# First modulation weights loaded ahead, and the start of the first layer put in another order: a fused two-layer hybrid block on one core

## The chip, the cores and the metric

The kernel runs on one core of a Trainium2 chip. Its time is device microseconds from one execution, and lower is better. Three executions of the kernel before gave 1947.54, 1946.19 and 1947.12 us, so the median is 1947.12 us. TensorE (PE in the profile, PEld for its weight loads) does the matmuls, VectorE is DVE, ScalarE is ACT, GpSimd is POOL, and SyncE is SP. SP and ACT issue the DMAs.

## The reference, cut to what matters

The network has two layers over 256 context tokens and 256 latent tokens of width 1024, all in float32. Each layer first makes its normalised input `h` and then feeds four mixers. The change touches only what is computed before the first projection of layer 0, so this is what matters:

```
mod   = silu(c)     @ w_ada[li] + b_ada[li]      # (6*1024): shift1, scale1, gate1, shift2, ...
mod_c = silu(c_ctx) @ w_ada[li] + b_ada[li]
h  = rmsnorm(x,  norm1[li]) * (1 + scale1)  + shift1
hc = rmsnorm(xc, norm1[li]) * (1 + scale1c) + shift1c
p, pc = h @ w_in[li], hc @ w_in[li]              # 1024 x 5648

# filter of the Hyena branch, per layer, orders n = 0, 1: depends on weights alone
hdn  = sin(freq0 * (feats @ w1 + b1));  hdn = sin(freq1 * (hdn @ w2 + b2))
taps = (hdn @ w3).reshape(256, 2, 2, 512) * decay        # both directions
taps = taps / sum(abs(taps), axis=0)
kf   = rfft(taps, n=512)
```

## The kernel before, in words

The activations of both streams lie transposed in SBUF, as `xT`: 8 blocks `k` of 128 channels by 512 tokens (context, then latent). A projection is done in strips: a strip is 512 rows by 256 columns of a weight matrix (512 KB), loaded by SP into one of four slots of `raw`, split by ACT (`split_hi`, L1535) and by DVE or POOL (`split_lo`, L1544) into a high and a low part in one of two slots of `whl`, and multiplied in three products (high by high, low by high, high by low; `mm3`, L660). So `h` too has a high and a low part, `hhl`. All other matmuls (L655) and the transposes through the identity (L760, L766) are plain float32. An order of the work is written out by hand for each engine; engines meet at semaphores, and each runs its own list in order. PSUM has eight banks: four `unit` banks and four `work` banks, which `fill` hands out in turn; `fill` waits until the consumer of the bank four fills before has given it back.

The start of layer 0 is `start_` on PE, ACT and DVE, then `norm(0, 0)`, then `dn(0)`, whose first twelve strips (`feature_strips`, L660) need `h`. In `start_` there are three pieces of work:

- The first eight modulation groups. A group `g` is 256 columns of `w_ada[0]`, all 1024 rows, loaded as two strips through the four slots of `raw`. `mod_group(0, g)` multiplies `csil` (the two conditioning vectors through SiLU) by both strips, in eight matmuls that use 32 columns of the array each. ACT copies the result to `modrow` (`mod_row`), PE transposes it (`mod_turn`, L760), and DVE reduces it into `mod` and adds the bias (`mod_cols`). There is one `modrow`, so the groups follow one another. `amps` makes the scale of the norm from groups 4 to 7.
- The activations: `stage` holds `ctx` and `x`; PE transposes them into eight fills and ACT copies these to `xT`. POOL squares seven of the eight blocks and adds them up (L3397, L3399), ACT squares the last, PE sums over the channels with two products by ones, and ACT makes `rstd`. `norm(0, 0)` then builds `hn` = x * amp * rstd: DVE the even blocks in one operation per stream (L2750), POOL the odd ones in two steps, the scale (L3405) and `rstd` (L3432). ACT adds the shift and rounds to the high part (L1783), DVE makes the low part (L2739). `h_ready` counts the blocks, and PE waits for it block by block in the first two strips.
- The filter of both orders `n` of layer 0: `filter_angles` (two small products, each followed by nine DVE operations and a sine), `filter_taps` (four products of 64 rows by 512 columns, with DVE's `filter_cut` behind), `filter_sums` (sums and differences of the directions, DVE), ACT's absolute values (`filter_taps` on ACT), `filter_scale` (four products by ones, and a reciprocal on DVE), `filter_spectrum` (eight products) and `filter_nyquist` (two). For order 1 the spectrum stands behind the norm and the last two products inside the first strips of `dn(0)`, at chunk 4 of `between`.

Rows of the biases, norms, convolutions and of `c` and `c_ctx` are loaded by SP and transposed together in `columns(li)` (L815, L817). SP loads first these rows, then the constants, then the modulation strips as slots come free, with `ctx` and `x` behind strip 3. ACT's queue loads the small filter operands at the very start and the three large filter tables (`hy_w3`, `decay`, the first part of `hy_table`) after the first `modrow` copy (L1816).

The lines that end the start, as they stand before:

```python
            start_()
            for li in range(DEPTH):
                norm(li, 0)
                if li == 0:
                    filter_spectrum(0, 1)
                dn(li)
```

Of the kernel before, what the change touches and what calls it, by code (L numbers as in the profile page):

```python
# [20 lines left out]
P = 128  # L21
# [99 lines left out]
def build(nc, x, c, ctx, c_ctx, w_ada, b_ada, norm1, norm2, w_in, attn_qk_gain, attn_lambda, attn_subln,  # L121
# [3 lines left out]
    with es:  # L125
# [33 lines left out]

        whl = sbr("whl", [P, RING, 2, KS, STRIP])  # L160
        hhl = sbr("hhl", [P, 2, KD, T])
# [98 lines left out]

        f_w1, f_w2, f_s, f_arg, f_turns, f_feats, f_inv = carve((P,), (P,), (L,), (L,), (L,), (L,), (BR_W,), at=6144)
# [36 lines left out]
        ROWS_DONE = [7 * 16, 5 * 16]  # L298
        HYW = 3 * 16
        HALF = L // 2 + 1  # L300
        FILTER_SMALL, FILTER_LARGE = 11 * 16, 3 * 16
# [73 lines left out]
        def qk_tile(li, which, m_):  # L375
            if which and li:
# [9 lines left out]
        hyf_loaded = sem("hyf_loaded")  # L386
# [5 lines left out]
        vm_loaded = [sem(f"vm_loaded{i}") for i in range(4)]  # L392
        unit_done = sem("unit_done")
# [8 lines left out]
                 "exp_ready a_ready aT_ready turns_ready odd_ready eo_ready anti_ready hyk_ready hyf_clear hyf_arg hyf_sin hyf_cut hyf_sums hyf_taps z_ready zf_ready hy_u fn_u fn_v "  # L402
# [35 lines left out]
        at_unit = at_mark = 0  # L438
# [104 lines left out]
        FIRST_MODS = 2 * D // STRIP  # L543
# [8 lines left out]
        add_mods(0, range(FIRST_MODS))  # L552
# [37 lines left out]
        def turn_bank(li, g):  # L590
            return unit_bank[first_unit[("mod", g), li] % UNITS][:, STRIP:2 * STRIP]
# [17 lines left out]
        def _(pe):  # L609
# [133 lines left out]
            def mod_group(li, g):  # L743

                assert first_strip[("mod", g), li] == n_strip[0]
                bank = fill(("mg", li, g)) if in_work_bank(li, g) else unit()
                for kh in range(2):
# [4 lines left out]
                    m.then_inc(filled if kh and in_work_bank(li, g) else unit_done, 1)  # L752
                if 0 < mod_place(li, g) < FIRST_MODS:
                    mod_turn(li, g - 1)
# [14 lines left out]
            def filter_angles(i):  # L769
                if i == 0:  # L770
                    pe.wait_ge(hyf_loaded, FILTER_SMALL)
                    b = fill(("f1",))
                    mm(b[:, 0:L], f_w1[0:HY_EMB, :], f_feats[0:HY_EMB, :]).then_inc(filled, 1)
                else:
                    pe.wait_ge(S["hyf_sin"], 1)
                    b = fill(("f2",))
# [20 lines left out]
            def filter_spectrum(li, n):  # L797
                z = f_z0[li][n]
                for fc in range(4):
# [12 lines left out]
            def columns(li):  # L812
                pe.wait_ge(rows_loaded[li], ROWS_DONE[li])
                b = fill(("cols", li))
                nc.tensor.transpose(b[:, 0:100], rows_of[li][0:100, 0, :], ident[0:100, 0:100])  # L815
                n = 52 if li == 0 else 36
                nc.tensor.transpose(b[:, 128:128 + n], rows_of[li][0:n, 1, :], ident[0:n, 0:n]).then_inc(filled, 1)  # L817

            def start_():
                pe.wait_ge(consts_loaded, 16)  # L820
                columns(0)
                filter_angles(0)
                pe.wait_ge(S["cT_ready"], 2)
                for g in range(FIRST_MODS):
                    mod_group(0, g)
                    if g == 0:
                        filter_angles(1)
# [9 lines left out]
                    if g == 4:  # L837
                        filter_scale(0, 0)
# [2782 lines left out]
```

## Time and profile before

| | |
|---|---|
| median of three runs | 1947.12 us (1946.19 to 1947.54) |
| span of the profiled execution, first to last instruction | 1946.3 us |
| PE busy over the span | 1873.7 us (96%) |
| DVE, ACT, POOL busy | 1284.9, 788.5, 608.5 us |
| mean granted clock of TensorE over the span | 0.987 |

The profiled execution is known only by its span; what lies around the span in a run is not listed for it. A row of the timeline gives start, duration, engine, line, operation, output<-input, shape and count, and in brackets the idle time before with what ended it. One float32 matmul stands as two records in the rows of L655. A granted clock of 1.00 is 2.4 GHz and 0.50 is 1.2 GHz.

### The profile page before, as it was taken

To read this page: it belongs to the slowest core of one execution; us is meant where nothing else is said; L and a number is where in the kernel's file an instruction comes from. 1 tells how busy PE (TensorE), PEld (TensorE's weight loads), DVE (VectorE), ACT (ScalarE), POOL (GpSimd) and SP (SyncE) were. 2 spreads that over 40 slices of the span, in tenths; PEclk is the share of its full clock that TensorE was granted. 3 is DMA by queue.
4 is the path that set the end of the run, shared out by engine and by line. 5 is a ranking of instruction groups with operands and counts; after the bars stand their busy time and mean duration, and the time that the engine had idled before them with its cause. 6 is when DMAs were issued, how large, how long until landed. Compare 5 with 4: busy or idle time off the path is not lost.

```text
span 1946.3 us, 32006 instructions
## 1 busy us (share of the span) xinstructions
PE 1873.7 (96%) x11146; PEld 1525.9 (78%) x11146; DVE 1284.9 (66%) x2122; ACT 788.5 (41%) x1627; POOL 608.5 (31%) x553
## 2 busy tenths in 40 slices
PE   6999899999999999999999999999998899999999
PEld 2556788767588888877888887787787789999999
DVE  4754867666856755358765776759686655567574
ACT  2325633356243333333222232356535545445453
POOL 3433243722312111163200223444555521143030
PEclk8999899999999999999999999999999999999999
DMA  6433111232234443344555556233214335554554
GB/s 226 139 107 105 38 56 55 87 121 80 84 130 152 130 161 118 95 134 160 185 173 186 174 194 196 87 87 87 77 44 136 104 109 176 177 168 156 180 183 140
DMA packets 210925, 252.98 MB, mean 130 GB/s; under 512 B 11715, under 2 KB 176900, under 8 KB 209796
## 3 DMA queue, kind: packets, MB, share of 16 engines
q1 hardware_dynamic: 207088, 235.01, 38.2%
q10 hardware_dynamic: 3732, 16.60, 2.3%
q8 instruction: 61, 1.00, 0.2%
q14 instruction: 44, 0.36, 0.1%
HBM read 245.29 MB, written 6.29 MB: 129 GB/s over the span
## 4 chain that ended last, share of the span: by engine, by line
PE 73%; issue 10%; DVE 8%; POOL 5%; ACT 4%; DMA 1%; ACTq 1%; DVEq 0%; POOLq 0%
PE psum L660 58%; PE psum L655 13%; POOL whl L1544 2%; DVE big L2570 2%; PE psum L766 1%; POOL big L3537 1%; ACT whl L1535 1%; ACT big L1783 1%; ACT big L1786 1%; PE psum L628 1%; DVE hhl L2739 1%; DVE big L2579 1%; POOL big L1634 1%; DMA big<-in_hy_table_dram 1%; DVE big L2722 1%
## 5 line engine op out<-in xcount | busy, mean ns | idle before, releaser
L660 PE MATMUL psum<-hhl,whl 128*128 128x512 f32 (+1 forms) x4416 | 826.6, 346 | 11.6 <-DVE hhl L2739 4.3
L660 PEld LDWEIGHTS psum<-hhl,whl 128*128 128x128 f32 x4416 | 693.3, 190 | 132.4 <-issue 24.8
L1535 ACT CAST whl<-raw 128x512 fp32r<-128x512 f32 x656 | 374.1, 618 | 811.6 <-PE psum L660 806.6
L1544 DVE TENSOR_TENSOR whl<-raw,whl 128x512 fp32r<-128x512 f32 x480 | 333.6, 736 | 315.3 <-ACT whl L1535 314.4
L660 PE MATMUL psum<-bigr,whl 128*128 128x512 f32 (+1 forms) x2688 | 474.9, 337 | 1.5 <-DVEq L3314 0.7
L660 PEld LDWEIGHTS psum<-bigr,whl 128*128 128x128 f32 x2688 | 412.8, 190 | 57.2 <-issue 2.2
L1544 POOL TENSOR_TENSOR whl<-raw,whl 128x512 fp32r<-128x512 f32 x176 | 233.6, 1349 | 377.5 <-ACT whl L1535 359.0
L655 PE MATMUL psum<-big 128*128 128x128 f32 (+8 forms) x1572 | 245.7, 326 | 17.9 <-DMA big<-in_hy_w_dram 5.4
L655 PEld LDWEIGHTS psum<-big 128*128 128x128 f32 (+4 forms) x1572 | 164.5, 175 | 77.3 <-issue 51.8
L3537 POOL TENSOR_TENSOR big<-big,tmp 128x512 f32<-128x512 f32 (+1 forms) x64 | 64.5, 1021 | 341.3 <-DVE tmp L3311 340.7
L660 PE MATMUL psum<-whl,hhl 128*128 128x512 f32 x672 | 160.1, 396 | 11.0 <-POOL whl L1544 9.1
L660 PEld LDWEIGHTS psum<-whl,hhl 128*128 128x128 f32 x672 | 125.6, 190 | 40.1 <-POOL whl L1544 12.2
L1786 ACT COPY big<-psum 128x512 f32<-128x512 f32 (+3 forms) x182 | 90.3, 497 | 131.3 <-PE psum L655 93.3
L1596 POOL TENSOR_TENSOR tmp<-tmp 128x512 f32<-128x512 f32 (+1 forms) x32 | 31.3, 979 | 320.1 <-ACT tmp L1783 320.1
L2722 DVE SCALAR_TENSOR_TENSOR big<-big,csil 128x512 f32<-128x512 f32 x112 | 87.9, 785 | 5.2
L1783 ACT ACTIVATE big<-psum 128x512 f32<-128x512 f32 (+3 forms) x142 | 65.9, 475 | 26.3 <-PE psum L655 10.8
L3405 POOL TENSOR_SCALAR big<-xT,amp 128x256 f32<-128x256 f32 x48 | 54.3, 1143 | 37.9 <-issue 26.7
L2703 DVE SCALAR_TENSOR_TENSOR big<-big,csil 128x512 f32<-128x512 f32 x84 | 64.4, 819 | 1.8 <-DVE tmp L3311 1.8
L2570 DVE TENSOR_TENSOR big<-psum,big 128x512 f32<-128x512 f32 (+2 forms) x74 | 47.5, 642 | 22.1 <-PE psum L655 19.1
L2574 DVE TENSOR_SCALAR big<-psum,cols 128x512 f32<-128x512 f32 (+1 forms) x48 | 31.8, 662 | 45.1 <-PE psum L660 27.0
L2579 DVE SCALAR_TENSOR_TENSOR big<-psum,cols,big 128x510 f32<-128x510 f32 (+1 forms) x96 | 58.4, 608 | 2.6
L1783 ACT ACTIVATE big<-psum,small 128x512 f32<-128x512 f32 (+2 forms) x72 | 40.8, 594 | 39.8 <-DVE small L2576 21.7
(187 smaller groups left out, 1524.9 us busy)
## 6 DMA issues: line engine op xcount, KB each, us to landing
raw<-in_w_mlp_dram SPq DMA_DIRECT2D x128, 512.0 KB, 3.8
raw<-in_w_in_dram SPq DMA_DIRECT2D x88, 512.0 KB, 3.7
big<-in_w_ada_dram SPq DMA_DIRECT2D x88, 512.0 KB, 5.1
raw<-in_w_gate_dram SPq DMA_DIRECT2D x64, 512.0 KB, 3.5
raw<-in_w_branch_dram SPq DMA_DIRECT2D x32, 512.0 KB, 3.5
raw<-in_w_ada_dram SPq DMA_DIRECT2D x24, 512.0 KB, 5.3
raw<-in_w_o_dram SPq DMA_DIRECT2D x16, 512.0 KB, 3.5
hy_spectra<-big ACTq DMA_DIRECT2D x2, 2560.0 KB, 9.3
```

The source lines that it names most:

```text
L655: return nc.tensor.matmul(o_, a, b, start=start, stop=stop)
L660: m = nc.tensor.matmul(o_, a(p_), b(q_), start=first and i == 0, stop=last and i == 2, skip_group_check=shared)
L1535: nc.scalar.copy(whl[:, r, 0, ks], raw_of(n)[:, ks]).then_inc(S["hi_ready"], 1)
L1544: ins = eng.tensor_tensor(whl[:, r, 1, ks], raw_of(n)[:, ks], whl[:, r, 0, ks].bitcast(F32), ALU.subtract)
L1783: return nc.scalar.activation(o_, i_, fn, **kw)
L1786: return nc.scalar.copy(o_, i_)
L2570: step(V.tensor_tensor(o_, a, b, op), s_)
L2579: step(V.scalar_tensor_tensor(o_, a, sc, b, op0, op1), s_)
L2703: V.scalar_tensor_tensor(um_acc[:, r, :] if k == 7 else um_part[:, r, :], um_raw[k // 2][:, k % 2, :], csil[:, k, r:r + 1], um_part[:, r, ...
L2722: ins = V.scalar_tensor_tensor(vm_acc if k == 7 else vm_part, w, c_, vm_part, MUL, ADD)
L3405: ins = G.tensor_scalar(hn[:, k, sl], xT[:, k, sl], amp[:, li, which, k, s_:s_ + 1], None, ALU.mult)
L3537: G.tensor_tensor(m_acc[:, i, tk], m_acc[:, i, tk], tmp[:, i % 2, tk], ALU.add)\
```

## The change

- The weights of the eight groups are loaded whole and ahead, into places that are unused until then: groups 0 and 1 as one transfer of 2 MB (512 columns, 1024 rows) into a part of the arena (where `hn` comes later), 2 and 3 into the memory of `whl`, 4 and 5 into the first half of `hhl`, 6 and 7 as two transfers of 1 MB into the rest of `hhl`. They no longer pass through `raw`. `mod_group(0, g)` becomes `first_mod(g)`.
- SP's list begins with the constants, `ctx` and `x`; the three filter tables are issued by SP among the modulation weights. The rows of both layers are issued by ACT's queue.
- `c` and `c_ctx` are loaded by ACT's queue into `tmp` and transposed on their own, ahead of all else on PE.
- The squares of all eight blocks are made by ACT into `raw`, and POOL only adds them. PE sums over the channels with one product, in the middle of the groups, and `rstd` is made there. The first two strips of `dn(0)` and groups 6 and 7 are loaded after that sum is done.
- The four absolute blocks of the taps of each order are added by POOL (`filter_added`), so that `filter_scale_added` has one product in place of four.
- A group's transposition (`mod_turn`) stands behind another piece of PE's work, not directly behind the next group.
- Both spectra of layer 0, and both `filter_nyquist`, are now on PE within `start_`; the one inside `dn(0)` goes.
- `first_norm` takes the place of `norm(0, 0)`: POOL multiplies the odd blocks by `rstd` before the last groups are there, and then scales and shifts them in one operation; the rest is as before.
- ACT's store of the first spectra (`keep_spectra(0)`) stands two steps later in `dn(0)`.

```diff
@@ PE @@
+            def first_mod(g):
+                bank = unit()
+                at, c0 = mod_part(g)
+                pe.wait_ge(mod_loaded[min(at, 3)], 16 if at < 3 else 32)
+                for k in range(KD):
+                    m = mm(bank[32 * (k % 4):32 * (k % 4) + 32, 0:STRIP], csil[:, k, :],
+                           mod_raw[at][:, k, c0:c0 + STRIP], k < 4, k >= 4)
+                m.then_inc(unit_done, 1)
+            def filter_scale_added(n):
+                pe.wait_ge(S["hyf_added"], n + 1)
+                mm(fill(("fs", 0, n)), ones, f_z1[0][n][:, 0, :]).then_inc(filled, 1)
             def start_():
                 pe.wait_ge(consts_loaded, 16)
+                pe.wait_ge(crow_loaded, 32)
+                nc.tensor.transpose(fill(("c",))[:, 0:16], crow, ident[0:16, 0:16]).then_inc(filled, 1)
+                filter_angles(0)
+                pe.wait_ge(x_loaded, 32)
+                for k in range(KD):
+                    b = fill(("x", k))
+                    turn(b, [stage[:, m, k * P:(k + 1) * P] for m in range(NT)]).then_inc(filled, 1)
+                filter_angles(1)
                 columns(0)
+                columns(1)
+                filter_taps(0, 0)
                 pe.wait_ge(S["cT_ready"], 2)
...
+                first_mod(0)
+                filter_taps(0, 1)
+                mod_turn(0, 0)
+                first_mod(1)
+                pe.wait_ge(S["sq_summed"], 1)
+                mm(fill(("ms", 0, 0)), ones, tmp[:, 1, :]).then_inc(filled, 1)
+                mod_turn(0, 1)
+                first_mod(2)
+                filter_scale_added(0)
+                mod_turn(0, 2)
+                first_mod(3)
+                filter_spectrum(0, 0, (0, 1))
+                mod_turn(0, 3)
+                first_mod(4)
+                filter_spectrum(0, 0, (2,))
+                mod_turn(0, 4)
+                first_mod(5)
+                filter_scale_added(1)
+                mod_turn(0, 5)
+                filter_spectrum(0, 0, (3,))
+                filter_nyquist(0, 0)
+                first_mod(6)
+                filter_spectrum(0, 1, (0,))
+                mod_turn(0, 6)
+                first_mod(7)
+                filter_spectrum(0, 1, (1,))
+                mod_turn(0, 7)
+                filter_spectrum(0, 1, (2, 3))
+                filter_nyquist(0, 1)
@@ PE, inside the strips of dn(0) @@
-                        if chunk == 4:
-                            filter_nyquist(0, 1)
@@ SP @@
+            sp.dma_start(stage[:, 0:2, :], ctx[0].rearrange("(m p) d -> p m d", p=P)).then_inc(x_loaded, 16)
+            sp.dma_start(stage[:, 2:4, :], x[0].rearrange("(m p) d -> p m d", p=P)).then_inc(x_loaded, 16)
...
+            load_first_mods(0)
+            load_filter_table(f_w3.rearrange("p a b -> p (a b)"), hy_w3.rearrange("l a b -> (l a) b"))
+            load_filter_table(f_decay.rearrange("p a b c -> p (a b c)"), decay)
+            load_first_mods(2)
+            load_filter_table(f_dft.rearrange("p a b -> p (a b)"), hy_table[:, 0:1024])
+            load_first_mods(4)
+            sp.wait_ge(S["sq_summed"], 1)
+            for n in range(2):
+                load_strip(first_strip["dn", 0] + n)
+            load_first_mods(6)
+            load_first_mods(7)
@@ ACT @@
             def start_():
                 load_filter()
-                act.wait_ge(S["cols_ready"], 1)
+                load_rows(0, act)
+                load_rows(1, act)
...
+                b = filled_bank(act, ("c",))
                 for s_ in range(2):
+                    step(f(csil[:, :, s_], b[:, 8 * s_:8 * s_ + 8], ACT.Silu), S["cT_ready"])
+                give_fill(act, ("c",))
+                for k in range(4):
+                    x_copy(k)
                 filter_sine(0)
+                for k in range(4, KD):
+                    x_copy(k)
+                x_square(0)
+                x_square(1)
+                filter_sine(1)
+                for k in range(2, KD):
+                    x_square(k)
+                log_exp_tables()
+                mod_row(0, 0)
+                mod_row(0, 1)
+                b = filled_bank(act, ("ms", 0, 0))
+                rsqrt(rstd[:], b, D, S["rstd_ready"], after=lambda: give_fill(act, ("ms", 0, 0)))
+                filter_taps(0, 0)
+                mod_row(0, 2)
+                filter_taps(0, 1)
+                for g in range(3, 7):
                     mod_row(0, g)
                 for i in range(RING):
                     split_hi(act, split_strips[i])
+                mod_row(0, 7)
@@ DVE: start_, from the cuts on @@
+                filter_cut(0, 0)
+                filter_cut(0, 1)
+                mod_cols(0, 0)
+                filter_sums(0, 0)
+                filter_sums(0, 1)
+                mod_cols(0, 1)
+                mod_cols(0, 2)
+                filter_scale(0, 0)
+                filter_spectrum(0, 0, (0, 1))
+                mod_cols(0, 3)
+                filter_spectrum(0, 0, (2,))
+                mod_cols(0, 4)
+                filter_scale(0, 1)
+                mod_cols(0, 5)
+                filter_spectrum(0, 0, (3,))
+                filter_nyquist(0, 0)
                 for i in range(RING):
                     split_lo(dve, split_strips[i])
+                filter_spectrum(0, 1, (0,))
+                mod_cols(0, 6)
+                filter_spectrum(0, 1, (1,))
+                mod_cols(0, 7)
+                amps(0, 0)
+                first_norm()
@@ POOL @@
+            def first_norm():
+                hn = HN[0]
+                for k in range(1, KD):
+                    pool.wait_ge(S["x_ready"], KD + k + 1)
+                    a = x_sq[:, 0, :] if k == 1 else tmp[:, 1, :]
+                    step(G.tensor_tensor(tmp[:, 1, :], a, x_sq[:, k, :], ALU.add),
+                         S["sq_summed"] if k == KD - 1 else pool_step)
+                filter_added(0)
+                pool.wait_ge(S["rstd_ready"], 1)
+                for k in range(1, KD, 2):
+                    ins = G.tensor_tensor(hn[:, k, :], xT[:, k, :], rstd[:], ALU.mult)
+                    if k == 1:
+                        step(ins)
+                        filter_added(1)
+                step(ins)
+                pool.wait_ge(S["amp_ready"], 1)
+                for k in range(1, KD, 2):
+                    for s_ in range(2):
+                        sl = slice(s_ * L, (s_ + 1) * L)
+                        ins = G.tensor_scalar(hn[:, k, sl], hn[:, k, sl], amp[:, 0, 0, k, s_:s_ + 1],
+                                              mod[:, 0, k, s_:s_ + 1], ALU.mult, ALU.add)
+                    ins.then_inc(S["hn_pool"], 1)
+            def filter_added(n):
+                pool.wait_ge(S["hyf_taps"], n + 1)
+                z = f_z1[0][n]
+                for i in range(1, 4):
+                    step(G.tensor_tensor(z[:, 0, :], z[:, 0, :], z[:, i, :], ALU.add),
+                         S["hyf_added"] if i == 3 else pool_step)
```

## Rows read from the trace of the kernel before

**Rows 1.** Part 1 of the page: busy time of each engine.
```profile
PE 1873.7 (96%) x11146; PEld 1525.9 (78%) x11146; DVE 1284.9 (66%) x2122; ACT 788.5 (41%) x1627; POOL 608.5 (31%) x553
```

**Rows 2.** Chain of waits, 0 to 160 us: start, duration, what.
```profile
19.45 10.03 DMA big<-in_hy_table_dram
...
42.52 26.67 issue
69.18 5.66 POOL big L3405 x5
```

**Rows 3.** Stretches of 5 us: busy PE, PEld, DVE, ACT, POOL; clock, DMA share, GB/s.
```profile
5.00:10.00 5.00, 0.71 (x2) 0.36 (x2) 1.04 (x6) 1.72 (x3) 0.00 (x0) 1.00 0.97 310
...
20.00:25.00 5.00, 4.51 (x31) 3.25 (x22) 2.87 (x10) 2.04 (x3) 0.00 (x0) 1.00 1.07 407
```

**Rows 4.** Timeline of PE, 0 to 70 us.
```profile
14.09 1.93 PE L655 MATMUL psum<-raw,csil 128*32 128x256 f32 x16
...
29.57 6.39 PE L655 MATMUL psum<-big 64*128 64x512 f32 x8 [1.08 <-DMA big<-in_hy_table_dram]
...
38.38 7.19 PE L655 MATMUL psum<-big 64*128 64x512 f32 x8
...
47.98 0.69 PE L760 MATMUL psum<-tab,rows 128*128 128x128 f32 x2
...
50.90 3.60 PE L655 MATMUL psum<-big,tab 128*128 128x512 f32 x8
54.43 1.07 PE L655 MATMUL psum<-raw,csil 128*32 128x256 f32 x16
...
57.08 8.75 PE L655 MATMUL psum<-big 128*128 128x512 f32 x20
```

**Rows 5.** Stretches of 1 us, PE alone: busy PE, granted clock, DMA share, GB/s.
```profile
50.00:51.00 1.00, 1.00 (x11) 0.58 0.88 268
...
200.00:201.00 1.00, 0.34 (x3) 1.00 0.81 285
201.00:202.00 1.00, 1.00 (x8) 0.51 0.47 178
```

**Rows 6.** Timeline of ACT, 0 to 80 us.
```profile
7.10 1.28 ACT L1783 ACT_TABLE_LOAD   x1 [7.10 <-issue]
...
25.06 5.47 ACT L1786 COPY xT<-psum 128x512 f32<-128x512 f32 x8
...
52.19 2.19 ACT L1783 ACTIVATE big<-big 128x512 f32<-128x512 f32 x4 [3.03 <-DVE big L2570]
```

**Rows 7.** Timeline of DVE, 0 to 80 us.
```profile
36.84 6.21 DVE L2570 TENSOR_TENSOR big<-big 128x512 f32<-128x512 f32 x4
...
49.23 2.87 DVE L2570 TENSOR_TENSOR big<-big 128x512 f32<-128x512 f32 x4
...
54.53 3.36 DVE L2615 RECIPROCAL big<-psum 128x512 f32<-128x512 f32 x1 [2.03 <-PE psum L655]
...
75.60 2.11 DVE L2750 SCALAR_TENSOR_TENSOR big<-xT,amp,rstd 128x256 f32<-128x256 f32 x4 [0.16 <-DVE big L2615]
```

**Rows 8.** Timeline of POOL, 0 to 80 us.
```profile
27.96 1.27 POOL L3399 TENSOR_TENSOR tmp<-tmp 128x512 f32<-128x512 f32 x1
...
37.80 1.59 POOL L3399 TENSOR_TENSOR tmp<-tmp 128x512 f32<-128x512 f32 x1
```

**Rows 9.** Timeline of all engines, 70 to 160 us.
```profile
69.18 9.31 POOL L3405 TENSOR_SCALAR big<-xT,amp 128x256 f32<-128x256 f32 x8 [26.68 <-issue]
...
79.62 1.95 PE L660 MATMUL psum<-hhl,whl 128*128 128x512 f32 x6
...
82.85 1.65 PE L660 MATMUL psum<-hhl,whl 128*128 128x512 f32 x6 [1.27 <-DVE hhl L2739]
...
85.46 11.20 PE L660 MATMUL psum<-hhl,whl 128*128 128x512 f32 x48 [0.96 <-DVE hhl L2739]
...
96.49 5.77 PE L655 MATMUL psum<-big 128*128 128x512 f32 x12
```

More of the change, by code:

```diff
@@ L392, in build @@
         vm_loaded = [sem(f"vm_loaded{i}") for i in range(4)]
+        mod_loaded = [sem(f"mod_loaded{i}") for i in range(4)]
         unit_done = sem("unit_done")
@@ L1829, in start_, with x_copy, x_square @@
                 load_filter()
-                act.wait_ge(S["cols_ready"], 1)
+                load_rows(0, act)
+                load_rows(1, act)
+                def x_copy(k):
+                    b = filled_bank(act, ("x", k))
+                    step(copy(xT[:, k, :], b), S["x_ready"])
+                    give_fill(act, ("x", k))
+                def x_square(k):
+                    step(f(x_sq[:, k, :], xT[:, k, :], ACT.Square), S["x_ready"])
+                b = filled_bank(act, ("c",))
@@ L1847, in start_ @@
+                for g in range(3, 7):
+                    mod_row(0, g)
                 for i in range(RING):
                     split_hi(act, split_strips[i])
+                mod_row(0, 7)
+                for k in range(KD):
+                    nm, count = hn_ready(0, k)
+                    act.wait_ge(S[nm], count)
+                    if k % 2:
+                        copy(hhl[:, 0, k, :], HN[0][:, k, :]).then_inc(S["hhi_ready"], 1)
+                        continue
+                    for s_ in range(2):
+                        sl = slice(s_ * L, (s_ + 1) * L)
+                        ins = f(hhl[:, 0, k, sl], HN[0][:, k, sl], ACT.Identity, bias=mod[:, 0, k, s_:s_ + 1])
+                    ins.then_inc(S["hhi_ready"], 1)
@@ L2616, in filter_scale, with filter_spectrum @@
                 give_fill(dve, ("fs", li, n))
-            def filter_spectrum(li, n):
+            def filter_spectrum(li, n, fcs=range(4)):
                 K = f_K[:, n]
-                for fc in range(4):
+                for fc in fcs:
                     b = filled_bank(dve, ("fk", li, n, fc))
@@ L3425, in norm @@
-                pool.wait_ge(S["rstd_ready"], n + 1)
-                if n:
-                    nm, count = hn_ready(n, 1)
-                    pool.wait_ge(S[nm], count)
-                if n:
-                    pool.wait_ge(S["h_ready"], KD * n + 1)
-                for k in range(3 if n else 1, KD, 2):
+                pool.wait_ge(S["amp_ready"], n + 1)
+                for k in range(KD):
+                    pool.wait_ge(S["x_added"], 24 * li + 8 * which - 7 + k)
+                    if k < KD - 2:
+                        squared(k)
+                    scaled(k, S["xa_ready"])
@@ L3551, in _ @@
                 if li == 0:
-                    norm(0, 0)
+                    first_norm()
                 enter(pool, ph(li, 0))
```

310 lines of the change are left out of this document (137 added, 173 removed).

## The prediction

> **What bounds the kernel now.** The busy times come first [rows 1]: PE is busy for 1873.7 of 1946.3 us, so as a whole it is PE's list that sets the end, and no other engine is above 66%. But that is an average. The change works on the first 100 us, so I read that stage next, in the chain of waits [rows 2]. The reader should see three links. PE waits until the last filter table lands (issued at 19.45, landed 10.03 us later, at 29.48). Then follow 26.67 us told as "issue" and POOL's scaling from 69.18, the way to the normalised input; PE has a full list of its own beside them. The stretches of 5 us say why the table is late [rows 3]: from 5 us on the DMA engines are used up (share about 1, 310 to 407 GB/s). At these rates some 9.4 MB have come in by 30 us: constants, `ctx`, `x`, eight modulation strips, the three tables. PE's timeline then shows that from 29.57 on PE works nearly without a gap [rows 4]. The last view is the first strips [rows 9]: the first product at 79.62, waits of 1.27 and 0.96 us for the low part of `h`, and dense products from 85.46. Twelve records were done by then, two steps of six, at 0.233 us each (11.20/48), so they are worth 2.8 us by those rows, or 2.57 at the 0.214 us that six products of 512 columns take back to back in a full strip. I take 2.57: before is as good as an uninterrupted start at 82.9. That is the number to beat.
>
> **TensorE's clock in this stage.** A modulation group takes 1.93 us at 14.09 and 1.07 us at 54.43 [rows 4]; the granted clock is 0.58 over 50 to 51 us, at the end of a stretch at 0.50, and full from there [rows 5]. So all of PE before about 50.8 us runs at 1.2 GHz, though the 5 us rows print 1.00 up to 30 us. A float32 product of 512 columns costs 0.86 us at 2.4 GHz (8.75/10, 3.60/4 with its latency) and 1.71 at 1.2 (6.84 for the four of a `filter_taps`, between 6.39 and 7.19). After a pause at 200 us (0.34 busy) the clock fell again at 201 [rows 5].
>
> **The change, step by step.**
>
> *Loads.* The bytes ahead of the last table are the same 9.4 MB; only their order changes, and they begin with SP's first instruction, some 2.5 us sooner, since the rows go to ACT's queue. At a mean near 385 GB/s (between the two rows, nearer the upper, which has large transfers alone [rows 3]) that is 24.4 us after a start near 2.6: the tables are there at **27.0**, in place of 29.5. Bounds: 25.5 at 407 GB/s, and 29.5 if nothing is gained.
>
> *What must be ready by then.* ACT issues 12 more small DMAs (rows twice five, `c`, `c_ctx`) ahead of its first table load, which stood at 7.10 [rows 6]; at about 0.4 us each it starts near 12.3. Then come table load, SiLU, copies and squares at 0.68 us each (5.47/8), two sines, each behind DVE's angle chain: second sine near 23, last square near 27, POOL's last add (1.27 to 1.59 us each [rows 8]) near 31.5. The sine has 4 us to spare against 27.0, the sum 13 us against the place where PE wants it. So I cost this at nothing; without that cover each us of it is one of PE's.
>
> *To the first sum of absolute taps.* PE, all at 1.2 GHz: taps 6.9, group 1.9, taps 6.8, transposition 0.65, group 1.9, the sum's product 1.7: 19.9 us, to 46.9. ACT then makes `rstd` (two operations of 0.68 and waits, 1.6) and takes four absolute values (2.19 [rows 6]): 50.7. DVE's eight sums and differences (2.87 for four [rows 7]) end earlier. POOL adds three times at 1.27 plus a gap of 0.08 [rows 8], 4.1 us: 54.8, say **55** with the signals. This wait is new. PE has only a transposition and group 2 left (2.6 us, to 49.5), and stands until 55: 5.5 us. Behind it on PE are the other transpositions, all later groups and every spectrum.
>
> *From there to the last transposition.* At 2.4 GHz: 14 spectrum and last-row products and 2 sums at 0.86 us are 13.7; five groups at 1.0 and six transpositions at 0.37 (spaced as at 54.43 and after) are 7.2: 20.9 us. DVE's reciprocals of 3.36 us [rows 7] lie beside that. After 5.5 us of standing I expect the clock to be down, as after the pause at 200 us, and to stay down while some 2 to 3.5 us worth of work is done at double time. I take 2.8: last transposition at 55 + 20.9 + 2.8 = 78.7. DVE has the two groups' columns, a spectrum block and the strips' low parts in between, and is 2 us behind: `amp` at 80.8.
>
> *To the first product.* PE has the last six products beside this, 5.2 us: 83.9. The first block of `h` takes two scaled halves, ACT's two halves and DVE's low part, 3.1 us: 83.9 too. After that PE takes 1.28 us a block, and DVE makes one in about 1.0. So an uninterrupted start at **84.0** against 82.9: +1.1 us. The new order removes seven products by ones (four times 0.86 at least are gone from PE, and the 3.2 us of POOL's scaling at the end), but it pays them back in the pause, in the clock, and in two groups that were done while PE waited for the tables before.
>
> *Inside dn(0).* The two products at chunk 4 go. That piece took 5.77 us for 12 records [rows 9]; eight records are 3.42. So **-2.35 us**. Bounds: -1.7 (products alone) and -3. `keep_spectra(0)` stands later, behind the gates' copy, with several us left before DVE needs the room: nothing, up to +2 if it is late.
>
> *Sum.* +1.1 - 2.35 = -1.25 us. The profiled span lies 0.8 us under the median, and I apply the difference to the median: 1945.9.
>
> **Two rules of the Trainium skill.** DVE's four sums took 6.21 us beside POOL's work and 2.87 without it, and POOL's add went from 1.27 to 1.59 [rows 7, 8]; DVE's scaled halves beside POOL's scaling lost little (2.11 for four). The Trainium skill, SBUF — State Buffer, section "Who interferes with whom", says that a DVE instruction with two SBUF inputs contends with a GpSimd one that reads SBUF, and that the loser blocks. By that rule all of `first_norm` takes turns; the trace agrees for tensor by tensor and hardly for POOL's scaling. The Trainium skill, TensorE: Matmul & The Clock Gate, section "What's actually happening", says that activity releases the throttle; by it the taps would soon run at full clock. Here 6.39 and 7.19 us of taps without a gap did not release it.
>
> **Rivals.**
>
> *The two engines take turns.* While POOL does its eight halves (9.31 us before, 0.92 to 1.2 each), each of DVE's operations waits for one. DVE's list is 20 operations, about 10.4 us. Eight of them, 3.8 us alone (0.475 each), then take 8 x (0.92 + 0.475) = 11.2, and the list 17.8. The last block has 1.2 us to spare, so the price is 7.4 - 1.2 = 6.2 us: 1945.9 + 6.2 = 1952. For it speak 6.21 against 2.87 [rows 7]; against it 2.11 for four [rows 7]. It makes the change slower than before from 2.5 us of blocked time on, which is its 1.2 us to spare and the gain of 1.25. Chance 0.12.
>
> *The clock is kept over the pause.* The 2.8 us go, and the DVE lag shrinks with them: 1943. For it: it had risen only just before. Against it: 201 us. Chance 0.15.
>
> *The taps run at full clock.* Eight products at 0.86 in place of 1.71 save up to 6.8 us: 1940. Against it stand both taps of before. Chance 0.06.
>
> *The tables come no sooner.* The transfers are no faster in the new order, or ACT's longer list is late: up to +2.5, so 1948.4, no change. Chance 0.15.
>
> *Forecast:* chance 0.52, own range 1943.5 to 1948.
>
> **How the numbers follow.** Predicted 1945.9, the likeliest case. The range 1940.5 to 1951 holds the kept clock, the late tables and most of the turns. What this measurement can tell from no change is 0.2%, 3.9 us. Faster by more (under 1943.2): the full-clock taps 0.06, half of the kept clock 0.08, and 0.10 of the forecast's lower edge with a start stage shorter than I count: 0.24. Slower (over 1951.0): the turns 0.11, and 0.03 from the late tables with something behind them: 0.14. Within: 0.62.
>
> **What would show it.** Right: the last table lands near 27; PE waits some 5 us for POOL after group 2, and the granted clock is 0.50 after that; first strip product near 84 with no waits between blocks; eight records at chunk 4. Wrong: taps at 0.43 us a record, waits on DVE's low part in the first strips, or a first product before 80 or after 88.

## The result, and the profile after

The changed kernel is slower. Five executions gave a median of 1952.41 us (1951.87 to 1953.51), against 1946.19 us (1943.89 to 1947.54) for five of the kernel before: a ratio of 1.0034, with a 95% interval of 1.0022 to 1.0046. Run again later, it gave 1.0036 (1.0023 to 1.0049). The ten executions together have a median of 1952.3 us; those of before in the later comparisons have 1945.4 us. So the loss is 6.9 us where a gain of 1.25 was forecast, and 1952.41 lies above the range, which ended at 1951.0.

The first views are of the changed kernel, in the order of the prediction's steps. SP's queue at the start (start, duration, what it issues, and where it is found):

```profile
2.92 3.04 SPq L1749 DMA_DIRECT2D big<-in_hy_w_dram  x1
...
6.87 0.87 SPq L1746 DMA_DIRECT2D whl_plain<-in_w_ada_dram  x1
7.78 9.52 SPq L1749 DMA_DIRECT2D big<-in_hy_table_dram  x1
```

The issue of the last filter table (`hy_table`) took 9.52 us, behind two transfers of 2 MB, and that of `hy_w3` (`in_hy_w`) 3.04 us, behind one. In the chain of waits the table landed at 29.02, not at 27.0:

```profile
7.78 21.24 DMA big<-in_hy_table_dram
```

PE's timeline shows the whole of it:

```profile
14.59 4.68 PE L788 MATMUL psum<-tab,big 128*128 128x128 f32 x24 [2.44 <-ACTq L1552]
19.11 0.60 PE L669 MATMUL psum<-big 128*128 128x256 f32 x2
...
29.11 7.16 PE L669 MATMUL psum<-big 64*128 64x512 f32 x8 [8.62 <-DMA big<-in_hy_table_dram]
...
38.07 7.19 PE L669 MATMUL psum<-big 64*128 64x512 f32 x8
...
47.67 1.83 PE L669 MATMUL psum<-tmp,tab 128*128 128x512 f32 x2
49.34 0.38 PE L782 MATMUL psum<-tab,rows 128*128 128x128 f32 x2
49.65 1.07 PE L669 MATMUL psum<-whl_plain,csil 128*32 128x256 f32 x16
57.40 2.08 PE L669 MATMUL psum<-big,tab 128*128 128x512 f32 x2 [6.68 <-POOL big L3558]
...
80.87 0.38 PE L782 MATMUL psum<-tab,rows 128*128 128x128 f32 x2
...
86.51 13.88 PE L674 MATMUL psum<-hhl,whl 128*128 128x512 f32 x60
100.33 3.70 PE L669 MATMUL psum<-big 64*128 64x512 f32 x8
```

The reader should see five things. The product at 19.11 took 0.60 us for its two records; the same product of the kernel before, at 18.20, took 1.22 (the row below). So TensorE had reached 2.4 GHz. Then it stood for 8.62 us for the table. The taps behind that took 7.16 and 7.19 us, half speed. PE stood again for 6.68 us for POOL's adds. And the strips of `dn(0)`, from 86.51 on, ran 60 records without a wait, where before had waits of 1.27 and 0.96 [rows 9].

```profile
18.20 1.22 PE L655 MATMUL psum<-big 128*128 128x256 f32 x2 [2.18 <-ACT big L1783]
```

The stretches of 5 us show the clock beside it (busy PE, PEld, DVE, ACT, POOL; granted clock, DMA share, GB/s):

```profile
20.00:25.00 5.00, 0.46 (x2) 0.27 (x2) 4.43 (x11) 2.56 (x5) 1.47 (x1) 1.00 1.01 390
25.00:30.00 5.00, 0.89 (x1) 0.50 (x2) 0.24 (x2) 4.71 (x7) 4.33 (x4) 0.52 1.04 393
...
45.00:50.00 5.00, 5.00 (x31) 2.02 (x34) 4.24 (x8) 0.77 (x2) 0.00 (x0) 0.59 0.82 203
50.00:55.00 5.00, 0.72 (x16) 0.15 (x8) 2.67 (x6) 4.79 (x10) 1.52 (x2) 1.00 0.01 2
55.00:60.00 5.00, 2.60 (x8) 1.14 (x12) 0.06 (x1) 0.88 (x2) 4.77 (x4) 0.60 0.00 0
```

The clock fell in the stretch from 25 us, while PE stood for the table, and came back in the one from 45 us. It fell again in the one from 55 us, while PE stood for POOL. Counted out, it was down for 23.9 and 6.8 us there, 30.7 us in all.

DVE and POOL at the end of the start, the place of the first rival:

```profile
53.40 3.95 POOL L3558 TENSOR_TENSOR big<-big 128x512 f32<-128x512 f32 x3 [19.99 <-ACT big L1830]
...
83.65 8.23 POOL L3549 TENSOR_SCALAR big<-big,amp,mod 128x256 f32<-128x256 f32 x8 [17.13 <-DVE amp L2649]
```

```profile
83.48 1.82 DVE L2757 SCALAR_TENSOR_TENSOR big<-xT,amp,rstd 128x256 f32<-128x256 f32 x4
```

POOL's eight scalings with shift took 8.23 us, 1.03 each, less than the 9.31 without the shift before [rows 9], and DVE's four scaled halves beside them 1.82 (2.11 before [rows 7]). The two didn't take turns here.

### The profile page after: what moved, and what is told of

Its sections match the earlier page's. It is cut to its first block, busy times and chain, and to the rows that moved or that the text cites. A ratio compares the mean times of both kernels' runs of the same rounds, so it can differ in the third digit from the quotient of the medians.

```text
span 1950.2 us, 31971 instructions
## 1 busy us (share of the span) xinstructions
PE 1872.4 (96%) x11133; PEld 1528.3 (78%) x11133; DVE 1280.1 (66%) x2118; ACT 791.9 (41%) x1630; POOL 607.5 (31%) x553
## 4 chain that ended last, share of the span: by engine, by line
PE 75%; issue 8%; DVE 7%; POOL 4%; ACT 3%; DMA 1%; SPq 0%; ACTq 0%; DVEq 0%; POOLq 0%
PE psum L674 58%; PE psum L669 14%; POOL whl L1583 2%; DVE big L2640 1%; DMA big<-in_hy_table_dram 1%; PE psum L788 1%; POOL big L3663 1%; ACT whl L1574 1%; PE psum L642 1%; DVE big L2649 1%; ACT big L1830 1%; ACT big L1833 1%; DVE hhl L2856 1%; POOL big L1673 1%; DVE big L2979 1%
## 5 line engine op out<-in xcount | busy, mean ns | idle before, releaser
L788 PE MATMUL psum<-tab,big 128*128 128x128 f32 x296 | 44.5, 292 | 10.8 <-DVE big L2649 3.5
## 6 DMA issues: line engine op xcount, KB each, us to landing
hy_spectra<-big ACTq DMA_DIRECT2D x2, 2560.0 KB, 10.2
```

Source lines behind the costliest of these rows:

```text
L788: m = nc.tensor.transpose(bank[:, i * P:(i + 1) * P], s, ids)
```

## How the executions are compared below

The clock isn't the same from one execution to the next, so one number of each profile is used throughout: when PE ends its piece at chunk 4 of `dn(0)`. The same 60 records of strips are done by then in every kernel. Before, that is 96.49 + 5.77 = 102.3 [rows 9]; in the changed kernel 100.33 + 3.70 = 104.0. "Half clock" is how long, in us, the profile shows a granted clock of 0.50, first up to 100 us and then from there to the end. The first 17 to 24 us aren't in it: there the profile prints 1.00 until the clock rises for the first time, though the durations are those of 1.2 GHz (1.22 us for the product at 18.20). "Span behind chunk 4" is the profiled span less the end of chunk 4.

| kernel | median us | chunk 4 ends | half clock up to 100 us; from there on | span behind chunk 4 |
|---|---|---|---|---|
| before, four profiles | 1945.4 | 102.3, 100.4, 101.8, 98.3 | 20.5, 10.2, 17.1, 6.8; after: 30, 27, 27, 30 | 1844.0, 1843.4, 1842.6, 1843.9 |
| changed, two profiles | 1952.3 | 104.0, 105.1 | 30.7, 37.5; after: 36, 22 | 1846.2, 1842.7 |
| tables first | 1950.9 | 103.0 | 34.1; 24 | 1844.5 |
| four products | 1952.3 | 102.7 | 27.3; 33 | 1847.6 |
| pause covered | 1948.8 | 101.3 | 23.9; 33 | 1848.4 |
| absolutes ahead | 1941.7 | 94.5 | 23.9; 31 | 1846.1 |
| tables' wait covered | 1943.0 | 95.8 | 10.2; 34 | 1844.9 |
| absolutes ahead and wait covered | 1937.4 | 88.3 | 0; 31 | 1847.0 |
| these two and tables first | 1939.0 | 91.7 | 3.4; 30 | 1843.1 |
| before, gaps covered | 1946.8 | 100.9 | 10.2; 27 | 1843.7 |

## The experiments

Where an expectation says how much of the loss lies in the start, it compares the first strip product or the end of chunk 4 with a profile of before.

**The kernel before, unchanged.** The clock of its start is the base of the whole sum, and was known from one execution.

> The kernel before once more, unchanged, for a second profile beside the times. Its profile had a span of 1946.3 us and the changed kernel's 1950.2, a difference of 3.9, while the medians differ by 6.2. Theory A, the start of the layer alone costs the time and the rest is spread between executions: this profile shows a span nearer 1944, with fewer or shorter stretches at 1.2 GHz than the 47 us of the first, and first strip products within 1 us of the first profile. Theory B, something later in the program differs as well: the span is again 1946 and the difference has to be found behind 250 us.

1944.37 us over 11 executions, span 1943.8, as theory A said. But the first strip product came at 77.75, 1.9 us sooner than in the first profile and not within 1 us of it, so this start differs too. Its half clock came in two pieces, of 6.8 and 3.4 us:

```profile
30.00:35.00 5.00, 5.00 (x8) 1.64 (x6) 2.08 (x3) 0.52 (x1) 4.69 (x5) 0.59 0.46 93
...
45.00:50.00 5.00, 5.00 (x36) 2.07 (x29) 3.86 (x9) 0.37 (x1) 0.00 (x0) 0.70 0.67 203
```

Two more executions of it were profiled later.

> The kernel before, unchanged, for its start's clock alone. So far its two profiles differ there: half clock 30.4 to 50.9 in the one (first strip product 79.6), 30.9 to 37.7 and 44.6 to 48.0 in the other (77.8). Theory A (the clock of its start varies between executions, and is often better than in the first profile): this one has less than 15 us of half clock in 25 to 70 us and its first strip product at 75 to 78 us. Theory B (the first profile is the rule): half clock for about 20 us from 30 us, first strip product at 79.6.

> The kernel before, unchanged, a fourth profile for the clock of its start. Theory A: less than 15 us of half clock in 25 to 70 us, first strip product at 75 to 78 us. Theory B: about 20 us of half clock from 30 us, first strip product at 79.6 us.

The one gave 1946.32 us, half clock for 17.1 us, first strip product at 79.06. The other gave 1944.12 us, 6.8 us and 75.68, with taps at full speed:

```profile
29.53 3.67 PE L655 MATMUL psum<-big 64*128 64x512 f32 x8 [0.89 <-DMA big<-in_hy_table_dram]
...
34.50 3.70 PE L655 MATMUL psum<-big 64*128 64x512 f32 x8
...
75.68 1.95 PE L660 MATMUL psum<-hhl,whl 128*128 128x512 f32 x6
```

So the same taps of the same kernel took 6.39 and 7.19 us in one execution [rows 4] and 3.67 and 3.70 in another. Theory A holds for the second of them; the first, at 79.1, is nearer to B. The first profile was the latest of four, and the mean of chunk 4's end is 100.7, 1.6 us sooner than in it.

**The tables first on SP.** This asks whether the late table is a matter of its place in the queue.

```diff
-            load_first_mods(0)
             load_filter_table(f_w3...); load_filter_table(f_decay...)
-            load_first_mods(2)
             load_filter_table(f_dft...)
+            load_first_mods(0)
+            load_first_mods(2)
             load_first_mods(4)
```

> The changed kernel with the three filter tables issued ahead of the modulation weights. Theory A, the late table is a full term: the table lands near 15 us in place of 29.0, the taps start when the second sine is ready, near 24.7 in place of 29.1, and all that follows up to the first strip product moves by 4.4 us, so 1952.4 - 4.4 = 1948.0. Theory B, the pause of PE behind group 2 is set by something else than PE's own order (ACT, POOL): the pause grows and the first strip product moves by under 2 us, 1951.

1950.92 us, ratio 1.0028 (1.0019 to 1.0038). The taps moved by 1.5 us, not by 4.4, since something else was next:

```profile
27.58 7.19 PE L669 MATMUL psum<-big 64*128 64x512 f32 x8 [3.78 <-ACT big L1830]
```

The small filter operands, in ACT's queue, had come later (DVE could use them at 17.34 in place of 13.89), and so the second sine. The first strip product came 1.0 us sooner (85.49). That is theory B's number and not its mechanism, for the pause didn't grow (6.58 us). The median fell by 1.4 us, which is less than the uncertainty of either kernel's ratio (1.9 and 2.5 us).

**Four products again, POOL's adds out.** Is the new wait for POOL the cause?

```diff
-                filter_scale_added(0)      # and (1); filter_added(0), (1) go from POOL
+                filter_scale(0, 0)         # and (0, 1)
```

> The changed kernel with the sums of the absolute taps of both orders made by four products on PE, as before, and POOL's additions gone. Theory A, the wait for POOL and the clock lost behind it make the loss: PE waits from 50.7 to about 53.4 in place of 57.4, the four products end near 57.2 in place of 59.4, and if the clock stays at 2.4 GHz the 3.4 us of half-speed work are saved too, less 1.5 us of extra products at the second sum: -4 us, 1948.4. If the pause of 2.7 us still costs the clock: -1, 1951.4. Theory B, the pause costs nothing since the first norm behind it is the limit: 1952.4.

1952.32 us, ratio 1.0033 (1.002 to 1.0046). The pause shrank from 6.68 to 2.59 us and the clock stayed up behind it, but each order has four products again in place of one:

```profile
53.45 3.70 PE L669 MATMUL psum<-big,tab 128*128 128x512 f32 x8 [2.59 <-ACT big L1830]
```

The first strip product came at 85.19, 1.3 us sooner than in the changed kernel, and the median didn't move. At five executions and an uncertainty of 2.5 us, 1.3 us can't be seen in the times. So POOL's adds by themselves aren't the loss. Without them PE still waits for ACT's absolutes, until 53.45, and then works 3.70 us in place of 2.08. What can be saved lies ahead of the absolutes.

**The pause covered.** Seven products that nobody reads keep TensorE busy while POOL adds, and nothing else moves.

```diff
                 first_mod(2)
+                cover(("pause", 0), 7)
                 filter_scale_added(0)
```

> The changed kernel with seven products by ones of no use (6.0 us) in PE's pause behind group 2, ahead of the product that waits for POOL. It takes the clock's part of the pause by itself: the wait for POOL ends at the same 57.4. Theory A: the clock stays at 2.4 GHz, the 6.8 us at half speed become 3.4, the first strip product comes 3 us sooner and the time is 1949.4. Theory B, the fallen clock is hidden by DVE's work in that stretch: 1952.4.

1948.75 us, ratio 1.0013 (1.0004 to 1.0022). The granted clock stayed at 1.00, where the changed kernel has 0.60:

```profile
55.00:60.00 5.00, 4.49 (x25) 1.68 (x25) 1.25 (x2) 0.98 (x3) 4.69 (x5) 1.00 0.00 0
```

Chunk 4 ended at 101.3 in place of 104.0 and 105.1, and the median fell by 3.5 us, as theory A said. So through the clock alone the pause costs some 3 us (2.7 and 3.8 at chunk 4).

**The changed kernel again.**

> The changed kernel once more, unchanged. Its five times (1951.9 to 1953.5) lie 7 us over 27 times of the kernel before (1945.2), while the start of the layer accounts for 1.8 us in the first pair of profiles and 3.8 against the second profile of before. If the start is all of it, more executions of the changed kernel bring its median down to 1949 to 1950.5, with a spread like that of the others. If something behind the start is also slower, it stays at 1952.4.

1951.35 us (1949.32 to 1954.98), ratio 1.0036. That lies between the two expectations, and the loss itself stands. Taps from 29.76, half clock for 27.3 and 10.2 us. All six profiles of this family in which the wait for the tables stands bare (the two of the changed kernel, and those of the tables first, four products, pause covered and absolutes ahead) have 23.9 or 27.3 us of half clock from there on.

**Sums and absolutes ahead.** This takes the pause away by order: DVE sums order 0 before it cuts order 1, and ACT takes the absolutes before the next row and `rstd`.

```diff
                 filter_cut(0, 0)
+                filter_sums(0, 0)
                 filter_cut(0, 1)
                 mod_cols(0, 0)
-                filter_sums(0, 0)
@@ ACT @@
                 mod_row(0, 0)
+                filter_taps(0, 0)
                 mod_row(0, 1)
                 rsqrt(rstd...)
-                filter_taps(0, 0)
```

> The changed kernel with DVE's sums of order 0 ahead of its cuts of order 1, and ACT's absolute values of order 0 ahead of the second modulation row and of rstd. Nothing is added or left out. Theory A, PE's pause behind group 2 is the length of the chain cuts, sums, rstd, absolute values, POOL: the absolute values are done near 42.5 and POOL near 46.5, ahead of PE at 50.7, so the 6.7 us of pause go, and the 3.4 us of clock behind it too, and the first strip product comes near 77 in place of 86.5: 1952.4 - 9.5 = 1943. Theory B, the engines behind the last group (DVE's columns, the build of h) are the limit: the first strip product moves by under 4 us, 1949.

1941.66 us (1940.12 to 1944.45, 11 executions), ratio 0.9982 (0.9973 to 0.9991): faster than before. POOL adds from 42.74 on, and PE no longer waits:

```profile
42.74 3.95 POOL L3558 TENSOR_TENSOR big<-big 128x512 f32<-128x512 f32 x3 [9.84 <-ACT big L1830]
```

```profile
29.41 7.16 PE L669 MATMUL psum<-big 64*128 64x512 f32 x8 [9.22 <-DMA big<-in_hy_table_dram]
...
50.45 1.13 PE L669 MATMUL psum<-big,tab 128*128 128x512 f32 x2
...
77.03 13.84 PE L674 MATMUL psum<-hhl,whl 128*128 128x512 f32 x60
```

Chunk 4 ended 9.5 and 10.6 us sooner than in the changed kernel, and the median is 10.6 us lower, near theory A's 9.5. The pause of 6.7 us and its clock (3.4 and 5.1 us in the two profiles) cover that. The half clock of the taps was still there (23.9 us).

**The wait for the tables covered.** Nine products that nobody reads, while PE stands for the table.

```diff
+                cover(("tables", 0), 9)
                 filter_taps(0, 0)
```

> The changed kernel with nine products by ones of no use (7.7 us) in PE's wait for the filter tables, from 20.5 us on. Theory A, TensorE had the full clock at 19 us (the second angle product took 0.60 us for two records) and lost it in the wait: the taps now take 3.6 us in place of 7.16, group 2 ends near 41 in place of 50.7, POOL's sum near 48 in place of 57.4, and the time is 1952.4 - 9.5 = 1943. Theory B, the taps with 64 rows let the clock fall whatever stands before them: the first taps gain at most 3.4 us and the rest nothing, 1949 to 1951.

1943.03 us (12 executions, 1937.48 to 1951.86), ratio 0.9992 (0.998 to 1.0004). The taps are no sooner, but twice as fast:

```profile
21.66 7.99 PE L642 MATMUL psum<-tab 128*128 128x512 f32 x18
29.63 3.67 PE L669 MATMUL psum<-big 64*128 64x512 f32 x8
...
48.96 2.08 PE L669 MATMUL psum<-big,tab 128*128 128x512 f32 x2 [7.39 <-POOL big L3559]
...
78.33 13.87 PE L674 MATMUL psum<-hhl,whl 128*128 128x512 f32 x60
```

Chunk 4 ended 8.2 and 9.2 us sooner, and the median is 9.3 us lower, as theory A said, though its executions spread over 14 us. The pause for POOL is still there (7.39 us).

**Both.**

> Both edits: absolute values ahead, and nine products of no use in the wait for the tables. Theory A: group 2 ends near 41 and POOL's sum near 42.5, the wait is under 2 us and the clock stays, the first strip product comes near 69 to 71: 1936. Theory B (the build of h and DVE are the limit once PE is fast): the first strip product comes near 75 and the gain over each edit alone is under 3 us, 1940.

1937.35 us (1931.91 to 1938.49, 6 executions), ratio 0.9951 (0.9939 to 0.9963). This beats both kernels: 8 us under before, 15 under the changed one. Theory A holds, with 70.75 for its 69 to 71. No half clock is left before 200 us, and PE waits for POOL for 2.25 us:

```profile
43.55 1.13 PE L669 MATMUL psum<-big,tab 128*128 128x512 f32 x2 [2.25 <-POOL big L3559]
...
70.75 13.88 PE L674 MATMUL psum<-hhl,whl 128*128 128x512 f32 x60 [0.75 <-DVE hhl L2771]
```

**The tables first as well.**

> The kernel with absolutes ahead and the table wait covered, and the filter tables issued on SP ahead of the first modulation weights, with 4 dummy products instead of 9 since the wait is shorter. With the tables first the taps waited for the second sine (27.6) and no longer for the tables (29.1 to 29.4). Theory A (the start's order alone decides, and the clock stays up): taps at 27.6 and at full clock, first strip product at 69 us, total 1935.7, 1.6 us under the one without this edit. Theory B (the modulation weights, 2 MB later in the queue, become the wait: first modulation product not before 37 us): total 1937 to 1940.

1938.96 us (1935.21 to 1941.96), ratio 0.9965 (0.9951 to 0.9978). Theory A fails, and B's mechanism too, though its number holds: the modulation weights weren't late (first product at 32.35). DVE shows what was. Its four sums of order 0, here (first) and in the kernel without this edit (second):

```profile
17.82 0.55 DVE L2647 TENSOR_SCALAR big<-psum,small 128x256 f32<-128x256 f32 x1 [12.75 <-DMA small<-in_hy_freq_dram]
...
33.30 5.74 DVE L2641 TENSOR_TENSOR big<-big 128x512 f32<-128x512 f32 x4
```

```profile
14.11 0.54 DVE L2647 TENSOR_SCALAR big<-psum,small 128x256 f32<-128x256 f32 x1 [9.16 <-DMA small<-in_hy_freq_dram]
...
33.90 2.87 DVE L2641 TENSOR_TENSOR big<-big 128x512 f32<-128x512 f32 x4
```

With the tables ahead of them in the DMA engines, the small operands (`hy_freq`) landed 3.7 us later. ACT's squares and POOL's adds of them moved with that, POOL's to 29.48 to 38.5, and lay over DVE's sums, which took twice as long:

```profile
29.48 9.01 POOL L3536 TENSOR_TENSOR tmp<-tmp,raw 128x512 f32<-128x512 f32 x6 [2.39 <-ACT raw L1831]
```

So the first rival's mechanism exists in this kernel, at another place. The Trainium skill, SBUF — State Buffer, section "Who interferes with whom", says that a DVE instruction with two SBUF inputs and a GpSimd one that reads SBUF contend; for tensor by tensor the runs agree (5.74 against 2.87), for POOL's scaling beside DVE's halves they show next to nothing (8.23 and 1.82).

**The kernel before with its short gaps covered.**

```diff
+                        cover(("start", 0), 1)      # before filter_angles(1)
...
+                                cover(("start", 1), 1)      # before the fifth turned block of x
...
+                        cover(("start", 2), 1)      # before filter_taps(0, 0)
```

> The kernel before with three dummy products of TensorE (table by table, each read by nobody) in the short gaps ahead of its taps: one before the second angle product, one in the middle of the turned x, one before the first taps. Theory A (what the kernel before keeps by chance is the clock of the taps; it is lost in about half of its executions): with the gaps shorter the taps run at full clock (4 records in about 2 us instead of 2.98 to 3.7), first strip product at 74 to 77 us, and the median is 1 to 4 us under the kernel before, at 1942 to 1944. Theory B (the clock in the start of the kernel before has nothing to do with what TensorE did in these gaps): 1945 to 1947, the dummy products costing about 1 us.

1946.80 us (11 executions), ratio 1.0002 (0.9993 to 1.0011), first strip product at 78.29. The numbers are theory B's. The taps did run at full clock, 1.5 us later than before, but one profile doesn't show that the covered gaps did it, since they ran so once in the unchanged kernel too. Then PE waited for DVE:

```profile
36.10 3.70 PE L655 MATMUL psum<-big 64*128 64x512 f32 x8
43.92 0.40 PE L815 MATMUL psum<-tab,rstd 100*128 100x100 f32 x1 [4.13 <-DVEq L1517]
```

The taps in half the time are worth little in this kernel, since DVE's cuts and sums are next, and the clock fell in that wait. Between the first and the last profile of before, PE's piece from the first taps to the second shrank by 7.3 us (from 16.0 to 8.7), and chunk 4 ended 3.9 us sooner.

## Why the prediction was wrong, step by step

*What bounds the kernel.* PE's list, and in the start its waits and its clock: right. The base was wrong. The 82.9 to be beaten came from the one execution at hand, and its clock was misread as well. "All of PE before about 50.8 us runs at 1.2 GHz" isn't what it shows: the 1.00 at 29 us was true, and the clock fell only inside the taps, 0.8 us after they had begun (stretches of 1 us: busy PE, granted clock, DMA share, GB/s):

```profile
29.00:30.00 1.00, 0.43 (x1) 1.00 1.11 353
30.00:31.00 1.00, 1.00 (x3) 0.68 1.09 285
31.00:32.00 1.00, 1.00 (x2) 0.50 0.62 137
```

That is why those taps took 6.39 us and the next 7.19. In four profiles that start is 1.6 us shorter on the mean than in the first. Together with the difference of the medians (1947.12 of three, 1945.4 of the later ones) the kernel before was a better one than the forecast took it for.

*Loads.* This step failed first. Tables at 27.0 were forecast from bytes and a mean rate; they landed at 29.02. Up to 29 us the engines moved 9.9 MB (29 us at 341 GB/s), 0.5 more than I counted, since groups 4 and 5, issued at 17.34, shared them with the table; that is 1.3 us at my 385 GB/s. The rest is the rate:

```profile
5.00:10.00 5.00, 1.40 (x3) 0.67 (x3) 0.00 (x0) 0.00 (x0) 0.00 (x0) 1.00 0.88 321
10.00:15.00 5.00, 2.38 (x10) 1.98 (x11) 0.93 (x3) 2.04 (x4) 0.00 (x0) 1.00 1.00 343
0.00:29.00 29.00, 9.21 (x41) 7.51 (x41) 8.86 (x26) 12.60 (x22) 5.07 (x8) 0.94 0.93 341
```

It was 321 and 343 GB/s in the two stretches from 5 to 15 us, where the forecast took 385 throughout. SP stood in the table's issue for most of that time; whether the one made the other isn't shown. The rival "the tables come no sooner" (27.0 + 2.0, for 0.5 us of gain in place of 2.5) is what happened, at a chance of 0.15; its time, 1948.4, lacked the rest.

*To the first sum.* Group 2 ended at 50.7 (49.5 forecast), POOL's adds at 57.35 (55). PE reached the sum's end at 49.5 (46.9): 2.0 us are the tables, the rest mostly the taps, which took 7.16 and 7.19 us (6.9 and 6.8). From there to POOL's last add it was 7.9 us, where 8.1 were forecast. The pause was 6.7 us (5.5) for another reason: the clock was back at 49.1, so PE did the transposition and group 2 in 1.2 us and not in 2.6. The new wait was seen and named, and sized 1.2 too small, but these 1.2 us didn't delay what comes after. What was wrong was to take the wait as the fixed price of the change. An order of DVE and ACT without it is 10.6 us faster, clock included. The forecast held the 8.3 us of pause and clock to be nearly paid for by what the new order saves elsewhere on PE, with +1.1 left.

*From there on.* The clock fell in the pause, and took 3.4 us (half of 6.8; 5.1 the second time) where 2.8 stood. From the end of the pause to the last transposition 23.7 us were forecast and 23.8 measured (57.40 to 81.2). That agreement is partly luck: 0.6 us more for the clock stand against 0.5 less for the work. The first strip product came at 86.51, 2.5 behind 84.0, of which the tables are 2.0. The strips had no waits, as forecast.

*Inside dn(0).* 5.77 us became 3.70: -2.1, forecast -2.35. Moving `keep_spectra(0)` was costed at nothing up to +2; it costs 0.4. ACT's issue of that store now stands ahead of the absolutes of layer 1, and PE waits:

```profile
118.74 0.36 ACTq L1969 DMA_DIRECT2D hy_spectra<-big  x1
119.15 3.51 ACT L1830 ACTIVATE big<-big 128x512 f32<-128x512 f32 x6 [0.52 <-ACT rstd L1833]
```

```profile
121.39 2.84 PE L669 MATMUL psum<-big,tab 128*128 128x512 f32 x6 [0.64 <-ACT big L1830]
```

*The sum.* The step that failed is the load and what it was held to cost: the tables were put at 27.0 and landed at 29.0, and the wait for them was priced at its own length, without the clock that was lost in it. Beside it the base of 82.9 was 1.6 us too late. Against the first profile of before, the end of chunk 4 was forecast at -1.25 and came at +1.8: +2.5 in the start (2.0 tables, the rest mostly the taps), +0.3 in the piece at chunk 4, and 0.2 because twelve records are worth 2.8 us, as the rows before said (13.82 for 60 here), and not the 2.57 that I took. No row shows its 0.214 us a product. The two profiles of after lie at 104.5 on the mean and the four of before at 100.7, so 3.8 of the 6.9 us are lost by chunk 4. That part is shown. Behind chunk 4 the same profiles differ by 1.0 us on the mean (1844.5 against 1843.5). Of it 0.4 is the store, and a stop of 1.0 us near 265 us, told as "issue", stands in both profiles of the changed kernel and in none of before, but also in some of the other orders and not in all. Half clock doesn't explain it: behind 100 us it is about 29 us on the mean in either kernel. The last 2 us of the 6.9 are in no profile, since the executions that were profiled lie nearer to each other than the medians do. Where they come from stays open.

*What was missed most.* The prediction took half clock for the taps as given, so a late table could only cost its own 2 us. But TensorE had the full clock before the table's wait (0.60 for the product at 19.11), and it was lost in the wait of 8.6 us. Before waited 1.08 us there [rows 4], began its taps at full clock in all four profiles, and lost it inside them in three. Products that nobody reads in that wait gave back 9.3 us, more than any term of the sum. The Trainium skill, TensorE: Matmul & The Clock Gate, section "Part 4: PE-mode transpose", says that in transpose mode the full clock doesn't engage; here 24 transposes through the identity, in 4.68 us, stand directly ahead of a product at full clock. Whether the program's transposes are that mode isn't shown by the rows. The third rival, taps at full clock for 1940, was the lever, with a chance of 0.06, and in the changed kernel it needed the gap closed, not more activity in the taps.

## What to carry to other kernels

Where a change moves work out of a wait to make it denser elsewhere, look at what is left in that wait: in this kernel TensorE stood for 8 us there and lost the full clock for the work behind it. A new wait between engines is first a question of order on the engine that feeds it: two moved calls on DVE and ACT were worth 10 us, more than the change they mended. And the clock of a stage is to be taken from several executions before it stands in a sum.

## What the runs showed of the hardware that was not expected

- SP's issue of a transfer stood for 9.52 us behind 2 MB transfers, and for 9.01 us in the order with the tables first, for the second 2 MB of modulation weights (the last but one of SP's transfers there):

```profile
4.59 9.01 SPq L1746 DMA_DIRECT2D whl_plain<-in_w_ada_dram  x1
```

- In the changed kernel PE worked without a gap from 29.11 us on (taps, a group, taps, a transposition, a group), and the clock was back only at 49.1 us. With the wait covered the same taps began at full clock and stayed there (3.67 and 3.70). Neither is a rule. In the kernel before, in three of four profiles, taps that began at full clock lost it within 2 us, and in one of these it was back at 37.7 us, after 6.8 us at half clock with taps and a group.
- The same kernel, unchanged, had 6.8 to 20.5 us of half clock in its start from one execution to another, and spans of 1942.2 to 1946.3.
